# Merges' last half units taken tile by tile, and the post norm rows made later in the output and down projections

## The reference

```python
# mixer sub-layer: three branches (retention, SSD, windowed attention), each 1024 wide
br = einsum('btnw,nwd->btnd', stack(outs, axis=2), w_branch)
g = sigmoid(gate_logits).reshape(..., 3, 1024)
merged = sum(g * br, axis=2)
y = merged @ w_out
x = x + mods_x[2] * rms_norm(y, n_post)
# feed-forward sub-layer (layer 0: SwiGLU; layer 1: top-2 of 8 experts)
y = (silu(h @ w1) * (h @ w3)) @ w2
x = x + mods_x[5] * rms_norm(y, n_post)
```

## Time and profile before

| | us |
|---|---|
| three runs, median | 2844.32 |
| three runs, lowest and highest | 2838.94, 2846.38 |
| profiled execution, its time | 2848.4 |
| profiled execution, its span | 2847.1 |
| TensorE busy | 2616.9 |
| VectorE busy | 1460.6 |
| ScalarE busy | 1298.6 |
| GpSimd busy | 763.1 |
| mean granted TensorE clock | 0.964 |

### The profile page before, as it was taken

One profiled execution on the slowest core, in us unless ns is written; L12 is line 12 of the kernel. 1 busy time (PEld: TensorE's weight loads), 2 busy tenths in 40 slices (PEclk: granted clock), 3 DMA queues, 4 the chain that ended last, 5 costly groups with the idle time before them and its releaser, 6 DMA issues. The chain is left out here.

```text
span 2847.1 us, 34994 instructions
## 1 busy us (share of the span) xinstructions
PE 2616.9 (92%) x13281; PEld 2129.2 (75%) x13281; DVE 1460.6 (51%) x1709; ACT 1298.6 (46%) x1677; POOL 763.1 (27%) x346
## 2 busy tenths in 40 slices
PE   6998999999998799998988898887799999999997
PEld 4775778877777688877765687656688888888885
DVE  2475321423522422202465225443788888888886
ACT  2570433331442322223553433344577677777765
POOL 0321443243223244433333545524100000000000
PEclk9989999999999899999989999999799999999998
DMA  6265232122112233322265433412799999999997
GB/s 228 75 222 192 89 89 75 60 89 84 50 53 96 67 95 89 103 75 89 74 191 177 120 89 105 132 60 75 270 361 344 332 372 355 332 351 360 352 326 278
DMA packets 234571, 496.55 MB, mean 174 GB/s; under 512 B 14864, under 2 KB 111408, under 8 KB 234288
## 3 DMA queue, kind: packets, MB, share of 16 engines
q1 hardware_dynamic: 232544, 494.20, 51.0%
q10 hardware_dynamic: 1872, 0.26, 0.1%
HBM read 493.37 MB, written 1.05 MB: 174 GB/s over the span
## 5 line engine op out<-in xcount | busy, mean ns | idle before, releaser
L290 POOL TENSOR_TENSOR unit_lo<-raw_units,unit_hi 128x1024 fp32r<-128x1024 f32 x244 | 590.1, 2440 | 1097.4 <-ACT unit_hi L282 1097.4
L2694 DVE TENSOR_TENSOR moe_unit_lo<-moe_raw,moe_unit_hi 128x2048 fp32r<-128x2048 f32 (+1 forms) x283 | 611.8, 2174 | 103.8 <-ACT moe_unit_hi L2688 100.8
L2688 ACT ACTIVATE moe_unit_hi<-moe_raw 128x2048 fp32r<-128x2048 f32 (+1 forms) x280 | 509.1, 1821 | 219.0 <-PE bank L311 218.2
L282 ACT ACTIVATE unit_hi<-raw_units 128x1024 fp32r<-128x1024 f32 x246 | 246.6, 1052 | 489.8 <-PE bank L311 400.6
L309 PE MATMUL bank<-unit_hi,hT_hi 128*128 128x256 f32 (+1 forms) x1168 | 421.8, 361 | 32.0 <-PEq L1347 13.7
L310 PE MATMUL bank<-unit_lo,hT_hi 128*128 128x256 f32 (+1 forms) x1168 | 400.4, 343 | 0.0
L311 PE MATMUL bank<-unit_hi,hT_lo 128*128 128x256 f32 (+1 forms) x1168 | 400.0, 342 | 0.0
L309 PE MATMUL bank<-moe_unit_hi,xe_T_hi 128*128 128x512 f32 (+1 forms) x768 | 290.4, 378 | 1.1 <-DVE xe_T_lo L2725 1.1
L310 PE MATMUL bank<-moe_unit_lo,xe_T_hi 128*128 128x512 f32 (+1 forms) x768 | 287.0, 374 | 0.0
L309 PEld LDWEIGHTS bank<-unit_hi,hT_hi 128*128 128x128 f32 x1168 | 227.0, 194 | 79.5 <-issue 43.1
L311 PE MATMUL bank<-moe_unit_hi,xe_T_lo 128*128 128x512 f32 (+1 forms) x768 | 286.3, 373 | 0.0
(11 more groups left out here) (401 smaller groups left out, 4171.9 us busy)
## 6 DMA issues: line engine op xcount, KB each, us to landing
moe_raw<-in_moe_w SPq DMA_DIRECT2D x224, 1024.0 KB, 7.3
raw_units<-in_w_in SPq DMA_DIRECT2D x160, 512.0 KB, 3.7
moe_raw<-in_moe_w SPq DMA_DIRECT2D x64, 768.0 KB, 4.3
ada_unit<-in_ada_w SPq DMA_DIRECT2D x40, 1024.0 KB, 5.2
raw_units<-in_ffn_w SPq DMA_DIRECT2D x66, 512.0 KB, 3.8
raw_units<-in_w_branch SPq DMA_DIRECT2D x48, 512.0 KB, 3.5
ada_first<-in_ada_w SPq DMA_DIRECT2D x8, 1024.0 KB, 13.9
raw_units<-in_w_out SPq DMA_DIRECT2D x16, 512.0 KB, 3.6
```

The lines of the kernel that those rows point to most:

```text
L282: act.activation(half_of(view(whi, g), half), half_of(view(raw, g), half), ACT.Copy).then_inc(hi_ready, 1)
L290: eng.tensor_tensor(lo, whole, hi.bitcast(F32), ALU.subtract).then_inc(lo_ready, 1)
L2688: act.activation(moe_hi[:, at_unit % RING, 0:n], moe_raw[:, at_unit % SLOTS, 0:n], ACT.Copy).then_inc(hi_m, 1)
L2694: dve.tensor_tensor(moe_lo[:, at_unit % SLOTS, 0:n], moe_raw[:, at_unit % SLOTS, 0:n], moe_hi[:, at_unit % RING, 0:n].bitcast(F32), ALU.su ...
```

## The change

It has three parts. In all six merges the last unit (second unit of column block 1) is multiplied tile by tile (`project_last`), each tile but the last increments a new semaphore `tile_done`, and VectorE waits for that tile alone. In `out_project` the rows product moves from the start to between the two units of the first column block and to banks 4 to 7, ScalarE's copies of it move behind its eight high parts, the first unit starts when four of the eight transposed pieces are split, and the wait for the copies moves ahead of the second column block. In `ffn_down` the wait for the copies moves into the first unit, which is taken tile by tile, tiles 2 and 3 (banks 4 to 7) ahead of it.

```diff
--- before.py
+++ after.py
@@ -1341,7 +1341,7 @@
             both = l == 1 and not whole
             m0 = a0
             part = at("merge_part", [P, 2, 512], F32, work + 16384)
-            gate_out, merged_out = stage_sem("gate_out"), stage_sem("merged_out")
+            gate_out, merged_out, tile_done = stage_sem("gate_out"), stage_sem("merged_out"), stage_sem("tile_done")
             n = len(tiles)
             a0 -= 0 if whole else 2
             with nc.Block() as block:
@@ -1381,8 +1381,11 @@
                 @block.vector
                 def _(dve):
                     for b in range(2):
-                        dve.wait_ge(unit_used, m0 + 2 * b + 2 if whole or both else a0 + 4 * b + 4)
                         for j, tile in enumerate(tiles):
+                            if b and j < n - 1:
+                                dve.wait_ge(tile_done, j + 1)
+                            else:
+                                dve.wait_ge(unit_used, m0 + 2 * b + 2 if whole or both else a0 + 4 * b + 4)
                             out = merged[:, tile, b * 512:(b + 1) * 512]
                             if whole:
                                 dve.wait_ge(gate_out, n * b + j + 1)
@@ -1402,18 +1405,26 @@
 
                 @block.tensor
                 def _(pe):
+                    def branch_products(g, b, banks):
+
+                        project_half(pe, g, 0, banks, tiles, outT)
+                        if b == 0:
+                            project_half(pe, g, 1, banks, tiles, outT)
+                        else:
+                            project_last(pe, g, banks, tiles, outT, lambda last, j: last.then_inc(tile_done, 1))
+
                     if whole:
                         for b in range(2):
-                            project(pe, a0 + 2 * b, [4 * b + j for j in range(n)], tiles, outT)
+                            branch_products(a0 + 2 * b, b, [4 * b + j for j in range(n)])
                     for b in range(2 if both else 0):
-                        project(pe, m0 + 2 * b, range(4 + n * b, 4 + n * b + n), tiles, outT)
+                        branch_products(m0 + 2 * b, b, range(4 + n * b, 4 + n * b + n))
                     for b in range(0 if whole or both else 2):
                         if b:
                             pe.wait_ge(gate_out, n)
                             project(pe, a0 + 4 * b, range(n), tiles)
                         if b:
                             pe.wait_ge(merged_out, n)
-                        project(pe, a0 + 4 * b + 2, [4 + j for j in range(n)], tiles, outT)
+                        branch_products(a0 + 4 * b + 2, b, [4 + j for j in range(n)])
             end_stage()
 
         def rope(dve, out, src, tile, table, n_heads, tmp, axial):
@@ -2247,9 +2258,9 @@
                 @block.scalar
                 def _(act):
                     split_hi(act, a0 + 1)
-                    post_rows_act(act, rows, conds, rows_sum, rows_out, [0, 1, 2, 3])
                     for f in range(KD):
                         outT_hi(act, tiles, f, turned, hi_out)
+                    post_rows_act(act, rows, conds, rows_sum, rows_out, [4, 5, 6, 7])
                     for g in range(a0 + 2, b0):
                         split_hi(act, g)
                     post.act_early(act)
@@ -2279,11 +2290,12 @@
 
                 @block.tensor
                 def _(pe):
-                    post_rows_pe(pe, l, 0, conds, rows_sum, rows_out, [0, 1, 2, 3])
-                    pe.wait_ge(rows_out, 2 * len(conds))
                     turn_to_outT(pe, merged, tiles, range(KD), None, turned, parts)
+                    pe.wait_ge(parts, 4)
+                    project_half(pe, a0, 0, range(n), tiles, outT)
                     pe.wait_ge(parts, KD)
-                    project(pe, a0, range(n), tiles, outT)
+                    post_rows_pe(pe, l, 0, conds, rows_sum, rows_out, [4, 5, 6, 7])
+                    project_half(pe, a0, 1, range(n), tiles, outT)
                     if routed:
                         for m in range(4):
                             column = (gains[l][:, 1, :, 0:1], mods[l][:, 24:32, 0:1])[m // 2]
@@ -2291,6 +2303,7 @@
                                 last = pe.matmul(ps[MOE_BANKS[m]][:, d * P:(d + 1) * P], column[:, 4 * (m % 2) + d, :].to_broadcast([P, P]),
                                                  ident, start=True, stop=True)
                             last.then_inc(moe_rows_sum, 1)
+                    pe.wait_ge(rows_out, 2 * len(conds))
                     for u, j in last_two(n):
                         pe.wait_ge(lo_ready, 2 * (a0 + 2 + u + 1))
                         w = [view(x, a0 + 2 + u) for x in (whi, wlo)]
@@ -2455,7 +2468,6 @@
                 @block.tensor
                 def _(pe):
                     post_rows_pe(pe, l, 1, [1, 0], rows_sum, rows_out, [0, 1, 2, 3])
-                    pe.wait_ge(rows_out, 4)
                     def down(g, k, tile, b):
                         kk = 2 * (g - a0) + k
                         wh, wl = view(whi, g), view(wlo, g)
@@ -2463,7 +2475,15 @@
                         return three(pe, ps[2 * tile + b][:, :], [x[:, kk, of_tile(tile)] for x in gT], [wh[:, k, s], wl[:, k, s]],
                                      kk == 0, kk == FT - 1)
 
-                    for g in range(a0, b0 - 2):
+                    pe.wait_ge(lo_ready, 2 * (a0 + 1))
+                    for tile in (2, 3, 0, 1):
+                        if tile == 0:
+                            pe.wait_ge(rows_out, 4)
+                        for k in range(2):
+                            for b in range(2):
+                                last = down(a0, k, tile, b)
+                    last.then_inc(unit_used, 1)
+                    for g in range(a0 + 1, b0 - 2):
                         pe.wait_ge(lo_ready, 2 * (g + 1))
                         for k in range(2):
                             for tile in ALL_TILES:
```

## The result

Eight runs of each kernel:

| | median us | lowest to highest |
|---|---|---|
| before | 2845.35 | 2838.94 to 2851.41 |
| changed | 2828.66 | 2823.81 to 2831.70 |
| ratio | 0.9937 | 95% interval 0.9924 to 0.9951 |

What follows compares the result with a forecast made beforehand. TensorE, busy 92% of the span, bounds the kernel, so time lies only where it idles or runs at half clock. Terms 12.8 + 2.7 + 3.8 - 1.0 + 0.7 = 19.0 us off the median 2844.32 gave 2825.3, range 2819 to 2836.

Steps and rivals of the forecast that it cites:

- retention, attention merge, layer 0: Joints behind these two merges: VectorE's tail shrinks from four tiles to one, saving 3.97 us each.
- SSM merge, layer 0: Joint behind this merge: one product is left of VectorE's four, saving 1.79 us.
- SSM merge, layer 1: Joint behind this merge: VectorE gets 0.59 us shorter, but SyncE is late next, so 0.42 us counts.
- retention, attention merge, layer 1: Joints behind these two merges: VectorE's tail shrinks from two tiles to one, 1.41 us, saving 1.33 us each.
- clock behind the retention merge: Stage after layer 0's retention merge: with idle time cut to 1.77 us the clock does not fall, returning 2.7 us.
- output projection, layer 0: First half unit starts 5.2 us in, not 12.76, with 3.7 us of rows between the halves: 3.8 us saved.
- output projection, layer 1: VectorE's router split holds the first half unit until 7.25 us; rows and clock cost more: 1.0 us lost.
- down projection: Start of the down projection: the wait for the last copy of the rows goes, saving 0.7 us.
- Held adds: Merges: tile 0's add is slowed beside GpSimd's split, 2.18 against 0.69 us; no cost taken, bound 1.5 us per layer 1 merge.
- rival 2: Layer 1 merges: tile 1's add is held too, so 2.66 us do not come; gain 16.4, time 2828; chance 0.07.
- The slower rival: Merges' last units: TensorE loses pace tile by tile; over 2852.9 us from 0.127 us per matmul; chance 0.03.
- rival 5: Layer 1's output projection starts with a full clock: 2.2 us more gain, time 2823; chance 0.04.

Runs made afterwards that it cites:

- ret_whole: The changed kernel, but in layer 0's retention merge VectorE waits for the whole last unit again: 2832.98 us, ratio 0.9964 to before.
- changed_3: The changed kernel itself, measured a third time with nothing altered: 2827.13 us, ratio 0.9936 to before.
- router_late: The changed kernel with VectorE's split of layer 1's router weights put behind its eight low parts: 2821.39 us, ratio 0.9919; measured again 2822.91 us, 0.9926.
- out_only: The kernel before with only the output projections changed: 2844.09 us, ratio 0.9997 to before.
- down_only: The kernel before with only the down projection changed: 2844.64 us, ratio 1.0001 to before.
- merges_only: The kernel before with only the merges changed: 2826.51 us, ratio 0.9943 to before.

## Why the prediction held, point by point

| step | forecast us | measured us |
|---|---|---|
| retention, attention merge, layer 0 | 3.97 each | 5.74 - 1.77 = 3.97 each |
| SSM merge, layer 0 | 1.79 | 3.18 - 1.39 = 1.79 |
| SSM merge, layer 1 | 0.42 | 1.64 - 1.35 = 0.29 |
| retention, attention merge, layer 1 | 1.33 each | 1.33, 1.32 |
| clock behind the retention merge | 2.7 | 2.5 (ret_whole: 1.7) |
| output projection, layer 0 | 3.8 | 4.07 |
| output projection, layer 1 | -1.0 | -1.74, and -0.2 in another profile |
| down projection | 0.7 | 1.2 |
| sum | 19.0 | 18.7 |

The clock's 2.5 us are read at the 48th matmul behind the joint, which starts 13.52 us after the first one before and 11.00 in the changed kernel.

The pair of profiles differs by 19.4 us, but that it comes so near to the sum is in part luck. Up to the end of layer 0's SSM merge, where no term lies, the changed profile is 3.5 us behind (382.6 against 379.1 us; 375.3 to 382.6 over all thirteen profiles), and stretches further on in which no term lies are shorter by 1.5 and 2.6 us and longer by 2.4. Together what lies outside the terms comes to 0.7 us. The medians differ by 15.1 to 17.1 in the three measurements, 2 to 4 us less than the profiled pair. Of the 3.4 us between the forecast of 2825.3 and the result, 1.0 is the median of before, which eight runs put higher than the three that the forecast had, 0.3 are the terms, and 2 us are open.

One part of them can be named. In six of the nine profiles with the short joint, changed_3 among them, the clock falls once more between 718 and 723 us, for 3.4 us, and the stretch up to the end of the next merge's matmuls is 1.5 us longer than in the other three; none of the four profiles with the long joint has that fall. The prediction counted the clock's return behind the joint and not what the clock does later in the same stage: of the 2.5 us, 1.0 is left at the stage's end in those six.

**Merges.** The reading of the earlier trace rows as VectorE's tail was right in all six. What became late next is as forecast: VectorE's work on the last tile in five joints, SyncE in layer 1's SSM merge. There the term was mis-sized by a little: from the end of SyncE's last issue to the next stage's first matmul pass 0.44 us (1573.81 to 1574.25), not the 0.32 that follow VectorE's last instruction.

**Held adds.** The mechanism was right in layer 1. Tile 0's add was held and the last tile was served in time, so the 2.66 us came and rival 2 is out. The timeline of layer 1's retention merge in the changed kernel, GpSimd first and then VectorE:

```profile
1766.89 4.76 POOL L290 TENSOR_TENSOR unit_lo<-raw_units,unit_hi 128x1024 fp32r<-128x1024 f32 x2 [0.50 <-ACT unit_hi L282]
```

```profile
1769.49 0.69 DVE L1403 TENSOR_TENSOR merge_part<-merge_gate,bank 128x512 f32<-128x512 f32 x1 [5.35 <-PE bank L311]
1770.22 1.99 DVE L1404 TENSOR_TENSOR merged<-merged,merge_part 128x512 f32<-128x512 f32 x1
1772.21 0.69 DVE L1403 TENSOR_TENSOR merge_part<-merge_gate,bank 128x512 f32<-128x512 f32 x1
```

The margin was small: TensorE's last matmul ended at 1772.17, the held add at 1772.21. In layer 0 the forecast of 2.9 us for tile 0's pair was wrong; the adds of the retention merge beside GpSimd took 0.71 (642.38 to 643.09) and 0.80 us (645.10 to 645.90), because a GpSimd instruction ended just then, at 642.54 and 645.35. The Trainium skill's "GPSIMD Engine Reference", section 1, Specifications, names the contention; the trace agrees, and it shows beyond it that what decides is when GpSimd's running instruction ends.

**Output projections.** Layer 0 came out as worked out, 5.09 against 5.2 and 3.73 against 3.7, and the low parts were not held by GpSimd. The queue behind the moved copies was hidden as forecast: GpSimd is through with the third unit 26.25 us into the stage and TensorE takes it at 30.59 (layer 1: 24.07 and 26.47), 4.3 and 2.4 us to spare against 4 and 2.6. In layer 1 the place and the moment were right (7.28 against 7.25) and the term for the clock was mis-sized: 2.2 us were taken between 1.7 and 2.7, and the first half unit with the rows takes 10.2 us in two profiles and 8.6 in the third, against 7.3 at clock 1.00 (router_late): 2.9 and 1.3 us lost. What the prediction did not ask is whether the router's split has to stand where it stands; moving it on top of the moved order gave 4.2 and 5 us, where the moved order alone (out_only) gave 2.3 in the trace and nothing that can be told in time. The router's split moved alone, in the order of before, was not run.

**The slower rival.** No pace was lost in the tile-wise order: the 48 matmuls of a last unit in layer 0 take 11.04 us in all three merges, before and after, and from 1766.44 to the end at 1772.17 the 24 of a last unit in layer 1 take 5.7 us, as before (1786.38 to 1792.14).

**Two sums of the prediction.** Rival 2 gains 19.0 - 2.66 = 16.3 us, not 16.4, and rival 5 less 3 us is 2820, not 2819. Neither changes anything.

**Clock elsewhere.** Between the joints the falls of the clock came to lie differently. The stretch from the down projection's second unit to layer 1's SSM merge is 2.6 us shorter in the changed kernel, the one from its retention merge to the end of its attention merge's matmuls 2.4 us longer (152.12 against 149.76), with three short falls in place of one longer one and much the same idle times. Both recur in nearly every profile of their side, but ret_whole, which has the changed code and one long joint, has the lengths of before (360.0 and 150.2 us), so it is not the code of those stretches that makes the difference. Why the falls lie where they lie was not tried.

## What to carry to other kernels

Where a stage ends with one engine working off all tiles, read one window over each stage end: an engine alone in it is time that a tile-wise release gives back, and if the idle time of TensorE there is long, its clock comes back on top (here 13 matmuls against 24 in 5.4 us); a part of that can go again in a later fall, so read the whole next stage and more than one profile. Moving work off a stage's start pays only where that work was last: ask for each stage what holds the first matmul, since in layer 1 it was an unrelated split on VectorE, and the moved rows only emptied TensorE ahead of its first half unit, with the half clock there for twice as long in two of three profiles.

## What the runs showed of the hardware

- An add of two SBUF tensors on VectorE that starts during a GpSimd instruction ends 0.55 us after that instruction's end, wherever it started: in the changed kernel 1772.20 after 1771.66, before 861.94 after 861.39. The GpSimd instruction that starts before such an add has ended takes 2.85 us in place of 2.40. A VectorE instruction with a PSUM operand is not held (0.69 us).
- Idle times of TensorE of 1.0 to 1.8 us at the merges' ends never brought its clock down in the joint or in the first 5 us behind it, in any of the twelve profiles of the changed kernel and the experiments or in the one before; 5.7 us always did, at seven joints of four profiles. Idle times of 3.1 to 3.2 us did so behind layer 1's attention merge in three of three profiles (before, out_only, down_only), and at the two other joints of that length in none of three. So the idle time alone does not decide. Nor does a fall need a long one: in merges_only the clock fell in the first half unit of layer 0's output projection, where the longest idle times ahead of it were 1.77 and 2.55 us.
